# A two-layer streaming step on one core: within-block GLA pairs as 32x32 products in one round, and a new order for the sample tile's turn

## The chip, the cores and the metric

The kernel runs on one core of one Trainium2 chip. The metric is the device time of one execution in microseconds (us), as the median of several runs. TensorE is called PE here, its weight loads PEld, VectorE DVE, ScalarE ACT, GpSimd POOL, and the engine that issues most transfers SP.

## The reference

The model is a step of a hybrid network: 1024 prompt tokens and 8 sampled streams of 16 tokens (1152 tokens, nine tiles of 128) pass through a layer with two recurrences (a gated delta rule and a GLA recurrence), a feed-forward block, a banded attention layer and another feed-forward block. The change touches the two recurrences alone, and of these mostly this part:

```python
def _gla(q, k, v, gk, s0):
    def step(s, inp):
        qc, kc, vc, gc = inp
        b = jnp.cumsum(gc, axis=2)
        o_inter = jnp.einsum('bhcd,bhde->bhce', qc * jnp.exp(b), s)
        diff = b[:, :, :, None, :] - b[:, :, None, :, :]
        decay = jnp.exp(jnp.where(causal[:, :, None], diff, -jnp.inf))
        a = jnp.einsum('bhid,bhjd,bhijd->bhij', qc, kc, decay)
        o = o_inter + jnp.einsum('bhij,bhje->bhie', a, vc)
        blast = b[:, :, -1:, :]
        s = (s * jnp.exp(blast[:, :, 0, :])[..., None]
             + jnp.einsum('bhcd,bhce->bhde', kc * jnp.exp(blast - b), vc))
        return s, o
```

There are 8 heads with 32 key channels and 64 value channels. The decay between two tokens is a product over channels, so `a` isn't one product of two matrices. The kernel splits it into levels.

## The kernel before

**Tiles and turns.** The stage of the recurrences is the function `recurrences`. It works on nine tiles of 128 tokens, the sample tile first (`order`, index 0), then the eight prompt tiles (1 to 8). It is a pipeline in which a turn i does three things at once: it inverts the triangular matrix of tile i and makes its GLA pairs, it prepares tile n = i + 1 (decays, transposes, q-k products), and it finishes tile s = i - 1 (values, outputs, states). The order on each engine is written out by hand in a function `turn`, with a `last_turn` for i = 8, and semaphores (`Tally`) join the engines. Turn 1 is the one in which the sample tile is finished (s = 0). It has eight states, one per stream, and reads them with many small products (`sample_reads`, L3582).

**The inverse.** Per turn there are four levels of blocks of 32: `z_blocks` (L3496) and `du_blocks` (L3503), each 32 products of 32x32, with a copy by ACT between them (`keep_z`) and a merge and a 32x32 transpose by DVE behind them (`put_level`, L4034 and L4036). Then come `z_quarters`, `du_quarters`, `z_half` and `du_half`, with `merge32` (L4046, L4048) and `merge64` (L4052) on DVE. `turn_w` (L3563) uses the finished inverse.

**The GLA pairs.** `exponents(n)` (L3479 to L3485) makes, for each of seven levels (distances 1, 2, 4, 8, 16, 32, 64), the sums of the log decays around a level's middle, and ACT takes their exponentials (`level_exps`). `level_queries` (DVE, L4125) and `level_keys` (POOL, L3395) scale q and k with them. `pairs(k, r)` (L3553) multiplies them in rounds: for each level and for the diagonal (`NL`), eight products of 32 rows, 128 columns of weights and 128 moving columns, one per head, into banks 4 to 7. `place(k, r)` (DVE) puts of each level's 128x128 result only the entries that belong to the level into `gla_pairs`: a masked copy of 128x1024 elements (L4093) for the levels up to 16 and for the diagonal, plain copies (L4090, L4087) for levels 32 and 64. A round holds two levels, as two fit in the banks, so `pairs` of round r + 1 waits for `place` of round r:

```python
rounds_p, rounds_s = [[0, 1], [2, 3], [4, NL], [5, 6]], [[0, 1], [2], [3], [NL]]
```

**The end of a turn** on PE reads: `pairs(i, 0)`, `du_quarters`, `turn_keys`, `turn_qk(n, 2)`, `turn_keys`, `z_half`, `pairs(i, 1)`, `du_half`, `a_pairs(n)`, `pairs(i, 2)`, `p_pairs(n)`, `pairs(i, 3)`, `turn_w`, `exponents(n)`. `turn_keys` (L3702) transposes keys of the attention cache that are on their way through the chip; SP loads and stores them. `smalls(n)` (L3429 to L3434) makes small sums, sixteen of its instructions being the total log decay per head (L3433).

**The stage ahead** is `rest_projection`, whose last group of nine row tiles (L2898) has the first steps of the sample tile between its products (`first_tile`). The first `exponents(0)` and `level_exps(0)` are in turn 0 of the recurrences.

Every fp32 product is two LDWEIGHTS and two MATMUL instructions; the profile counts them singly. An fp32r product is one of each.

Of the kernel before, what the change touches and what calls it, by code (L numbers as in the profile page):

```python
# [21 lines left out]
P = 128  # L22
# [8 lines left out]
GK = 32  # L31
# [20 lines left out]
def shape_constants():  # L52
# [11 lines left out]
    for s in LEVELS:  # L64
# [11 lines left out]
                               for s in LEVELS[:5]], 1)  # L76
# [2505 lines left out]
class FirstTile:  # L2582
# [3 lines left out]
    def __init__(self, load, scale, sums, turn_gla, turn_qk, a_pairs, p_pairs, decays, keep_gla, keep_qk, keep_blocks, factors,  # L2586
                 tiles):
        self.load, self.scale, self.sums, self.turn_gla, self.turn_qk = load, scale, sums, turn_gla, turn_qk
        self.a_pairs, self.p_pairs, self.decays, self.keep_gla, self.keep_qk = a_pairs, p_pairs, decays, keep_gla, keep_qk
        self.keep_blocks, self.factors, self.tiles = keep_blocks, factors, tiles  # L2590


def first_tile(e, ctx, at_):
# [11 lines left out]
    def own(name, shape, spot, dt=F32):  # L2605
# [29 lines left out]
     gla_turned, gla_ready, turned, tready, a_mm, bt_ready, p_mm, pt_ready, btc_ready, zeroed, uc_set, u_put, t_ready) = e.sem(  # L2635
# [3 lines left out]
        "first_p_mm", "first_pt_ready", "first_bt_blocks", "first_zeroed", "first_blocks_set", "first_u_put", "first_t_ready")  # L2639
# [86 lines left out]

    def decays(act):
# [28 lines left out]
    def factors(dve):  # L2756
# [5 lines left out]
        v.tensor_copy(spr[:, 8 * P:9 * P], c("upto_s"))  # L2762
# [19 lines left out]
    return FirstTile(load, scale, sums, turn_gla, turn_qk, a_pairs, p_pairs, decays, keep_gla, keep_qk, keep_blocks, factors,  # L2782
# [3 lines left out]
def rest_projection(e, ctx, hT, raw, out, ws_first, base, done, begin):  # L2786
# [43 lines left out]

    def bank(n):
        return PS[:, 5 + n % 3, :]
# [60 lines left out]
    def tensor(pe):  # L2893
# [22 lines left out]
        def first_step(t):  # L2916
# [9 lines left out]
            if t == 7:  # L2926
                begin.p_pairs(pe)

# [7 lines left out]
        for b in range(4):  # L2936
            for t in range(3 if b == 0 else 0, NT):
                pe.wait_ge(copied, b * NT + t - 2)
# [108 lines left out]
def recurrences(e, ctx, at_, ahead, first):  # L3047
# [11 lines left out]
    rounds_p, rounds_s = [[0, 1], [2, 3], [4, NL], [5, 6]], [[0, 1], [2], [3], [NL]]  # L3059
# [42 lines left out]
    ga = sb("gla_pairs", [P, 2, H, P])  # L3102
    qt = sb("qT", [P, 3, H // 2, P])
# [49 lines left out]
    pairs_mm, ga_put = tally("gla_pairs_mm", 4), tally("gla_pairs_put", 4)  # L3153
# [177 lines left out]
    def gpsimd(pool):  # L3331
# [15 lines left out]
        def scale(k):  # L3347
# [6 lines left out]
            upto = c("upto_s" if sample(k) else "upto_p")  # L3354
# [10 lines left out]
        def decay(k):  # L3365

            if sample(k):
# [5 lines left out]
                go_mm.wait(pool, k)  # L3373
                for m in range(2):
                    x = tt_(GSs[:, m], GSs[:, m], wide(exl[:, k % 3, m], DK), ALU.mult)
                x.then_inc(gsd_ready.sem, 1)
# [12 lines left out]

        def level_keys(k):  # L3390
# [7 lines left out]
        def turn(i, n, s):  # L3398
            if s is not None:
                decay(s)  # L3400
            if n is not None:
                scale(n)
# [9 lines left out]
    def tensor(pe):  # L3412
# [329 lines left out]
        def turn(i, n, s):  # L3742
            if i == NT - 1:
                return last_turn(i, s)
# [1506 lines left out]
```

## Time and profile before

| What | us |
|---|---|
| Median of 3 runs | 3221.96 |
| Lowest and highest run | 3221.78 and 3223.81 |
| The profiled execution | 3232.05 |
| Its span | 3230.4 |

PE is busy 3093.9 us of the span (96%), its weight loads 2905.2 us, DVE 1578.8, POOL 1527.5, ACT 1029.4. The recurrences take from 439.8 us to about 882 us of the span. In the rows of a timeline, the columns are the start, the time from the first start to the last end, the engine, the source line, the operation with its operands and shape, the number of instructions, and in brackets how long the engine stood idle before it and what released it. A row groups instructions of one kind that follow each other.

### The profile page before, as it was taken

How to read it: one execution, taken by the hardware profiler on the slowest of the kernel's cores; microseconds unless marked ns; L12 is line 12 of the kernel's file. 1: busy time of each engine (PE TensorE's matmuls, PEld its weight loads, DVE VectorE, ACT ScalarE, POOL GpSimd, SP SyncE). 2: the span in 40 equal slices, each digit the busy share in tenths (PEclk: the TensorE clock that was granted, in tenths of full speed). 3: DMA queues.
4: the chain of work that ended last, by engine and by line, in shares of the span. 5: the costliest groups of instructions: out<-in, count | busy, mean ns of one | idle time of the engine just before them, and what ended most of it. 6: DMA issues, size and time to landing. Idle time of an engine off the chain costs nothing. (4 is left out here: it accounts for less than half of the span.)

```text
span 3230.4 us, 67257 instructions
## 1 busy us (share of the span) xinstructions
PE 3093.9 (96%) x28484; PEld 2905.2 (90%) x28484; DVE 1578.8 (49%) x2177; ACT 1029.4 (32%) x1834; POOL 1527.5 (47%) x1163
## 2 busy tenths in 40 slices
PE   7999987888898999999999999999999999999999
PEld 6988876777798999999999999877699999999998
DVE  5650034565566545554334433466646445553323
ACT  4222132333434332231212432356624332231112
POOL 4452324344115776674363556311126766764352
PEclk8999988999898999999999999999999999999999
DMA  6222142432651322236423353567521333238342
GB/s 208 83 79 98 59 135 65 146 127 98 212 188 56 97 99 79 94 120 255 146 94 138 93 155 116 171 212 240 155 77 64 103 97 103 78 111 303 98 141 79
DMA packets 371080, 409.45 MB, mean 127 GB/s; under 512 B 29048, under 2 KB 303569, under 8 KB 369768
## 3 DMA queue, kind: packets, MB, share of 16 engines
q1 hardware_dynamic: 363944, 380.24, 35.5%
q0 software_dynamic: 6848, 25.04, 2.5%
q8 instruction: 222, 3.64, 0.5%
q14 instruction: 66, 0.54, 0.1%
HBM read 272.71 MB, written 134.60 MB: 126 GB/s over the span
## 5 line engine op out<-in xcount | busy, mean ns | idle before, releaser
L864 PE MATMUL PS<-token_block,w_block 128*128 128x288 f32 x9408 | 1272.3, 297 | 13.6 <-POOL w_block L778 6.5
L864 PEld LDWEIGHTS PS<-token_block,w_block 128*128 128x128 f32 x9408 | 1264.0, 190 | 16.2 <-POOL w_block L778 6.1
L778 POOL TENSOR_TENSOR w_block<-w_pair_raw,w_block 128x512 fp32r<-128x512 f32 x224 | 303.2, 1360 | 163.2 <-ACT w_block L774 129.2
L1259 PE MATMUL PS<-act_slot,w_down_split 128*128 128x384 f32 x1872 | 330.4, 337 | 6.6 <-DMA act_slot<-act_dram 5.5
L1259 PEld LDWEIGHTS PS<-act_slot,w_down_split 128*128 128x128 f32 x1872 | 328.1, 189 | 8.2 <-DMA act_slot<-act_dram 6.4
L778 POOL TENSOR_TENSOR w_block<-w_sum,w_block 128x512 fp32r<-128x512 f32 x168 | 228.7, 1376 | 96.9 <-ACT w_block L774 96.8
L774 ACT CAST w_block<-w_pair_raw 128x512 fp32r<-128x512 f32 x224 | 137.7, 622 | 306.6 <-PE PS L864 265.2
L774 ACT CAST w_block<-w_sum 128x512 fp32r<-128x512 f32 x168 | 99.5, 621 | 366.2 <-POOL w_sum L767 235.6
L1231 PE MATMUL PS<-token_block,w_block 128*128 128x288 f32 x1344 | 180.4, 296 | 2.1 <-issue 2.1
L1231 PEld LDWEIGHTS PS<-token_block,w_block 128*128 128x128 f32 x1344 | 179.4, 189 | 3.0 <-issue 2.5
L762 POOL TENSOR_TENSOR w_sum<-w_pair_raw 128x512 f32<-128x512 f32 x56 | 87.9, 1570 | 166.4 <-DMA w_pair_raw<-in_ffn_w_gu_dram 112.0
L405 PE MATMUL PS<-hT_high,w_split_tiles 128*128 128x384 f32 x576 | 124.9, 342 | 2.6 <-DVEq L2468 2.6
L1090 POOL CAST w_down_split<-w_down_raw 128x1024 fp32r<-128x1024 f32 (+2 forms) x32 | 28.1, 878 | 207.7 <-PE PS L1259 172.6
L1555 DVE TENSOR_TENSOR xT<-xT,PS 128x1152 f32<-128x1152 f32 x32 | 43.3, 1354 | 155.5 <-PE PS L1259 155.5
L1481 DVE TENSOR_TENSOR u<-p,PS 128x576 f32<-128x576 f32 x44 | 33.1, 752 | 164.9 <-PE PS L864 164.9
L4968 ACT ACTIVATE probs<-minus_scores,minus_max 128x640 f32<-128x640 f32 (+3 forms) x144 | 101.3, 707 | 23.5 <-DVE minus_max L4857 23.2
L1546 DVE TENSOR_TENSOR xT<-xT,PS 128x576 f32<-128x576 f32 x72 | 52.6, 752 | 106.3 <-PE PS L1231 106.3
L3395 POOL TENSOR_TENSOR gla_k_exps<-gla_exps,gla_kT 128x896 f32<-128x896 f32 x18 | 37.1, 2083 | 142.3 <-ACT gla_exps L3820 142.3
L405 PEld LDWEIGHTS PS<-hT_high,w_split_tiles 128*128 128x128 f32 x576 | 101.4, 190 | 2.9 <-POOLq L2338 2.9
L5005 POOL COPY bias_samples<-bias_near 128x384 f32<-128x384 f32 x16 | 8.1, 504 | 195.7 <-DMA bias_near<-near_dram 171.9
L764 POOL TENSOR_TENSOR w_sum<-w_sum,w_pair_raw 128x512 f32<-128x512 f32 x56 | 98.4, 1757 | 4.4
L1497 DVE TENSOR_TENSOR ffn_up<-ffn_up,norm_row 128x1152 f32<-128x1152 f32 x44 | 94.1, 2138 | 4.6
(520 smaller groups left out, 5516.3 us busy)
## 6 DMA issues: line engine op xcount, KB each, us to landing
w_pair_raw<-in_ffn_w_gu_dram SPq DMA_DIRECT2D x88, 512.0 KB, 5.1
act_slot<-act_dram SPq DMA_DIRECT2D x28, 1152.0 KB, 13.0
cache_kT<-kT_dram SPq DMA_DIRECT2D x8, 2048.0 KB, 11.6
cache_v<-in_cache_c_v_dram SPq DMA_DIRECT2D x64, 256.0 KB, 4.8
act_dram<-ffn_act_high SPq DMA_DIRECT2D x28, 576.0 KB, 2.8
act_dram<-ffn_act_low SPq DMA_DIRECT2D x28, 576.0 KB, 3.9
down_source<-down_dram SPq DMA_DIRECT2D x56, 288.0 KB, 5.2
xT<-xT_dram SPq DMA_DIRECT2D x24, 576.0 KB, 12.0
```

The lines of the kernel that those rows point to most:

```text
L405: m = nc.tensor.matmul(PS[:, banks + j, 0:GN], wl if p == 2 else wh, sl if p == 1 else sh, start=(k == first and p == 0), stop=(k == last ...
L762: tt(self.sum_(p, 2), b0, b1, ALU.add).then_inc(self.summed, 1)
L764: tt(self.sum_(p, 1), self.sum_(p, 2), a0, ALU.subtract).then_inc(self.summed, 1)
L774: self.nc.scalar.copy(self.blocks[q][:, 0], self.source(p, q)).then_inc(self.high, 1)
L778: self.nc.gpsimd.tensor_tensor(self.blocks[q][:, 1], self.source(p, q), self.blocks[q][:, 0], ALU.subtract).then_inc(self.low, 1)
L864: m = nc.tensor.matmul(to[:, j], w, x[:, j * HN:(j + 1) * HN], start=(q < 3 and i == 0 and t == 0), stop=(q > 3 and i == 3 and t == 2), sk ...
L1231: m = nc.tensor.matmul(to[:, j], w, x[:, j * HN:(j + 1) * HN], start=(q < 3 and i == 0 and t == 0), stop=(q > 3 and i == 3 and t == 2), sk ...
L1259: m = nc.tensor.matmul(down_banks(u)[:, j], wd[u % 2][:, int(q == 2), k], x[:, int(q == 1), group(j)], start=(k == 0 and q == 0), stop=(k ...
L1497: tt(up[:], up[:], row[:], ALU.mult).then_inc(up_scaled, 1)
L1546: tt(two(x), two(x), down_tile(d, q), ALU.add).then_inc(x_down, 1)
L1555: tt(groups(xT[:, n]), groups(xT[:, n]), down_banks(u), ALU.add).then_inc(x_added, 1)
L4968: nc.scalar.activation(pr[:, g % 2, hp, 0:w], sc[:, hp, 0:w], ACT.Exp, scale=-1.0, bias=mn[:, g % 2, hp, 0:1], accum_out=sm[:, g % 2, hp, ...
```

## The change

Five things change, all in the recurrences and the step before them.

1. **Pairs as blocks.** For the levels 1 to 16 and the diagonal only tokens within the same block of 32 matter. Their products are cut into 32x32 blocks: per level 2 x 4 x 4 = 32 products of 32 rows, 32 weight columns and 32 moving columns instead of 8 products of 32x128x128. Six such levels fit in the banks, so there are two rounds instead of four. DVE merges them by six masked copies of 128x256 into a small tile `gla_pair_blocks` (`gc`), and ACT copies that into the diagonal blocks of `gla_pairs` (`spread_pairs`, four copies of 32x256). The outputs wait for it.
2. **Order of the prompt turns.** `pairs(i, 2)` and `pairs(i, 3)` are gone; `turn_w` stands between `a_pairs` and `p_pairs`.
3. **A turn of its own for the sample tile** (turn 1) on PE, ACT and DVE: the prompt tile's `dec_sums` and `smalls` come between the sample tile's reads of its states; the masked values (`vm`) are made by ACT instead of DVE; the GLA states are multiplied by their decay later in POOL's order.
4. **First exponents.** `exponents(0)` goes to the end of `rest_projection`, behind the last row tile; the last three row tiles use banks 0, 3 and 0.
5. **Small things.** The total log decay per head is one product with ones instead of eight; two of DVE's first fills come later in turn 0.

```diff
-    rounds_p, rounds_s = [[0, 1], [2, 3], [4, NL], [5, 6]], [[0, 1], [2], [3], [NL]]
+    rounds_p, rounds_s = [[0, 1, 2, 3, 4, NL], [5, 6]], [[0, 1, 2, 3], [NL]]
...
         def pairs(k, r):
...
-                    for h in range(4):
-                        rows = slice(GK * h, GK * h + GK)
-                        w, q = (gkt[:, k % 2, m], gqt[:, k % 2, m]) if j == NL else (kl[:, m, j], ql[:, m, j])
-                        y = mm(PS[:, 4 + h, x * 256 + m * P:x * 256 + (m + 1) * P], w[rows], q[rows], start=True, stop=True)
+                    w, q = (gkt[:, k % 2, m], gqt[:, k % 2, m]) if j == NL else (kl[:, m, j], ql[:, m, j])
+                    if j in (NL - 2, NL - 1):
+                        for h in range(4):
+                            rows = slice(GK * h, GK * h + GK)
+                            y = mm(PS[:, 4 + h, x * 256 + m * P:x * 256 + (m + 1) * P], w[rows], q[rows], start=True, stop=True)
+                        continue
+                    for b in range(B):
+                        for h in range(4):
+                            rows = slice(GK * h, GK * h + GK)
+                            y = mm(PS[quad(b), 4 + h, (x * 2 + m) * Q:(x * 2 + m + 1) * Q], w[rows, quad(b)], q[rows, quad(b)],
+                                   start=True, stop=True)
...
         def place(k, r):
...
                 else:
-                    mask = c("up")[:, j * P:(j + 1) * P].rearrange("p (a b t) -> p a b t", a=1, b=1)
-                    y = v.copy_predicated(to, bc(mask, (P, 4, 2, P)), src)
+                    n = min(j, 5)
+                    mask = c("upc")[:, n * Q:(n + 1) * Q].rearrange("p (a b t) -> p a b t", a=1, b=1)
+                    src = PS[:, 4:8, x * 2 * Q:(x + 1) * 2 * Q].rearrange("p h (m t) -> p h m t", m=2)
+                    y = v.copy_predicated(within, bc(mask, (P, 4, 2, Q)), src)
...
+        def spread_pairs(k):
+            ga_put.wait(act, k, 1 if not sample(k) else 2)
+            for b in range(B):
+                x = copy(ga[quad(b), k % 2, :, quad(b)], gc[quad(b)])
+            x.then_inc(ga_spread.sem, 1)
...
         def turn(i, n, s):                      # PE, end of a prompt turn
...
             if n is not None:
                 a_pairs(n)
-            if i is not None:
-                pairs(i, 2)
-            if n is not None:
+            if n is not None and i is not None:
+                turn_w(i)
                 p_pairs(n)
-            if i is not None:
-                pairs(i, 3)
-                turn_w(i)
             if n is not None:
                 exponents(n)
...
+        def sample_turn(i, n, s):               # PE
+            z_blocks(i, 0)
+            sample_values(s)
+            dec_sums(n)
+            du_blocks(i, 0)
+            smalls(n)
+            sample_q_state(s)
+            z_blocks(i, 1)
+            turn_keys(i, 0)
+            du_blocks(i, 1)
+            outputs(s)
+            z_blocks(i, 2)
+            gla_turn(n)
+            du_blocks(i, 2)
+            sample_gla_outputs(s)
+            z_blocks(i, 3)
+            turn_qk(n, 0)
+            sample_dn_states(s)
+            du_blocks(i, 3)
+            turn_keys(i, 1)
+            sample_gla_states(s)
+            z_quarters(i)
+            turn_qk(n, 1)
+            pairs(i, 0)
...
         def smalls(k):
...
-            for h in range(H):
-                r, m = dn_rows(h)
-                mm(PS[r, 3, 16 + m * nb:16 + (m + 1) * nb], gt[:, h:h + 1].broadcast_to((P, DK)), ends, start=True, stop=True)
+            mm(PS[:, 3, 2 * H:3 * H], e.ones, gt, start=True, stop=True)
...
+            if t == 8:                          # PE, rest_projection, behind its last row tile
+                begin.exponents(pe)
...
+            if i == 0:                          # DVE, turn 0, behind put_level(0, 2)
+                v.memset(ga[:], 0.0).then_inc(zeroed, 1)
```

## Rows read from the trace of the kernel before

**Rows 1.** The page: engines' busy time, and the DMA queue of instructions (packets, MB).

```profile
PE 3093.9 (96%) x28484; PEld 2905.2 (90%) x28484; DVE 1578.8 (49%) x2177; ACT 1029.4 (32%) x1834; POOL 1527.5 (47%) x1163
...
q8 instruction: 222, 3.64, 0.5%
```

**Rows 2.** Windows by turn (0, 1, 3, 8): length, busy times (instructions), granted clock, DMA.

```profile
439.79:483.60 43.81, 38.13 (x843) 30.78 (x843) 26.20 (x33) 17.21 (x34) 21.14 (x19) 0.73 0.75 212
483.60:549.64 66.04, 50.04 (x1441) 42.10 (x1439) 31.25 (x47) 17.36 (x36) 23.75 (x19) 0.79 0.25 78
...
594.23:638.66 44.43, 38.73 (x961) 33.16 (x959) 26.75 (x42) 17.28 (x35) 19.55 (x15) 1.00 0.37 122
...
816.43:882.40 65.97, 56.48 (x1021) 51.32 (x1020) 38.13 (x58) 27.96 (x43) 10.59 (x7) 0.79 0.65 216
```

**Rows 3.** Timeline of PE in turn 3.

```profile
594.23 0.75 PE L3496 MATMUL PS<-inverse_blocks,minus_aT_blocks 32*32 32x32 f32 x64
595.61 1.97 PE L3621 MATMUL PS<-v_beta,inverse_T 128*128 128x64 f32 x16 [0.63 <-ACT gla_exps L3820]
...
603.18 0.63 PE L3433 MATMUL PS<-consts_f,dn_log_decay 128*64 128x1 f32 x16
...
619.16 1.17 PE L3553 MATMUL PS<-gla_q_exps,gla_k_exps 32*128 32x128 f32 x32 [0.46 <-DVE gla_state L4162]
...
624.37 1.11 PE L3526 MATMUL PS<-inverse_first_half,minus_aT_odd 64*64 64x64 f32 x16
...
636.42 0.50 PE L3479 MATMUL PS<-spans_r,gla_g_split 128*128 128x512 f32 x1 [0.66 <-DVE gla_pairs L4087]
```

**Rows 4.** Waits of PE in turns 2 to 7: total us, times, longest.

```profile
PE PS L3553 <- DVE gla_pairs L4093: 11.7, 12, 1.4
PE PS L3479 <- DVE gla_pairs L4087: 4.0, 6, 0.7
```

**Rows 5.** Timeline of DVE in turn 3.

```profile
606.45 0.44 DVE L4034 COPY_PREDICATED inverse_T_blocks<-consts_u,PS 128x256 f32<-128x256 uint8 x1
...
622.95 0.83 DVE L4046 COPY inverse_T<-PS 32x256 f32<-32x256 f32 x2
...
629.77 1.20 DVE L4058 SCALAR_TENSOR_TENSOR minus_aT_even<-PS,decay 128x1024 f32<-128x1024 f32 x1
...
635.68 0.68 DVE L4087 COPY gla_pairs<-PS 64x512 f32<-64x512 f32 x1
```

**Rows 6.** Timeline of ACT in turn 3.

```profile
631.00 1.65 ACT L3889 COPY minus_aT_blocks<-minus_aT_even 32x256 f32<-32x256 f32 x4 [4.91 <-DVE minus_aT_even L4058]
```

**Rows 7.** Timeline of PE in turn 1.

```profile
491.38 1.17 PE L3582 MATMUL PS<-dn_states,sample_qT 64*32 64x64 f32 x96 [2.11 <-issue]
492.48 0.58 PE L3496 MATMUL PS<-inverse_blocks,minus_aT_blocks 32*32 32x32 f32 x32
495.39 0.65 PE L3496 MATMUL PS<-inverse_blocks,minus_aT_blocks 32*32 32x32 f32 x32 [2.33 <-issue]
...
527.14 2.09 PE L3553 MATMUL PS<-gla_q_exps,gla_k_exps 32*128 32x128 f32 x32
```

**Rows 8.** DMA of 484 to 500 us: GB/s in 40 slices of 0.4 us; the only queue.

```profile
GB/s 0 0 41 0 0 0 0 0 0 0 0 0 41 0 0 0 0 0 0 0 0 0 41 0 0 0 0 0 0 0 0 41 0 0 0 0 0 0 0 0
...
q8 instruction: 4, 0.07, 1.7%
```

**Rows 9.** A window of 6 us in turn 1, columns as in rows 2.

```profile
493.00:499.00 6.00, 3.67 (x42) 1.99 (x37) 5.70 (x7) 0.37 (x1) 4.76 (x4) 0.50 0.02 5
```

**Rows 10.** Timeline of PE, turn 0.

```profile
439.79 0.74 PE L3496 MATMUL PS<-inverse_blocks,minus_aT_blocks 32*32 32x32 f32 x64 [3.55 <-DVEq L4298]
...
446.85 0.75 PE L3496 MATMUL PS<-inverse_blocks,minus_aT_blocks 32*32 32x32 f32 x64 [1.04 <-DVE inverse_blocks L4036]
```

**Rows 11.** Timeline of PE, turn 8.

```profile
828.54 0.64 PE L3496 MATMUL PS<-inverse_blocks,minus_aT_blocks 32*32 32x32 f32 x50 [0.30 <-issue]
...
833.29 0.31 PE L3503 MATMUL PS<-inverse_T_blocks,z_blocks 32*32 32x32 f32 x11 [0.73 <-issue]
```

More of the change, by code:

```diff
@@ L3353, in scale @@
             tt_(kb[:], kk, wide(col(e.rkb, k), DK), ALU.mult).then_inc(scaled.sem, 1)
-            upto = c("upto_s" if sample(k) else "upto_p")
+            if between:
+                between()
+            upto = c("upto_p")
             dec_exp.wait(pool, k)
@@ L3401, in turn @@
             if n is not None:
-                scale(n)
+                scale(n, (lambda: decay_sample_gla(s)) if s is not None and sample(s) else None)
                 if n + 1 < NT:
@@ L3415, in dec_sums @@
         def dec_sums(k):
-            after = c("after_s" if sample(k) else "after_p")
+            after = c("after_p")
             ug_ready.wait(pe, k)
@@ L3736, in last_turn @@
             ahead.turn(pe, 0)
-            pairs(i, 2)
-            pairs(i, 3)
             turn_w(i)
             ahead.turn(pe, 1)
+        def sample_turn(i, n, s):
[22 more added lines that the diff above has]
+            pairs(i, 0)
+            du_quarters(i)
+            turn_qk(n, 2)
+            turn_keys(i, 2)
+            z_half(i)
+            pairs(i, 1)
+            du_half(i)
+            a_pairs(n)
+            turn_w(i)
+            p_pairs(n)
+            exponents(n)
         def turn(i, n, s):
@@ L3744, in turn @@
                 return last_turn(i, s)
+            if s is not None and sample(s):
+                return sample_turn(i, n, s)
             if i is not None:
                 z_blocks(i, 0)
-            if i == 0:
-                exponents(0)
             if s is not None:
-                (sample_values if sample(s) else values)(s)
+                values(s)
             if i is not None:
@@ L3761, in turn @@
                 du_blocks(i, 1)
-            if s is not None and not sample(s):
+            if s is not None:
                 state(s)
@@ L3970, in turn @@
                 return last_turn(i, s)
+            if s is not None and sample(s):
+                return sample_turn(i, n, s)
             if i is not None:
@@ L4214, in turn @@
                 return last_turn(i, s)
+            if s is not None and sample(s):
+                return sample_turn(i, n, s)
             if i is not None:
@@ L4237, in turn @@
                 factors(n)
-            if s is not None and not sample(s):
+            if s is not None:
                 add_gla_state(s)
```

173 lines of the change are left out of this document (115 added, 58 removed).

## The prediction

> **What bounds the kernel now.** I first read the page: PE is busy 96% of the span [rows 1], so time is won only where PE stands idle or does less. The windows, one per turn of the recurrences, come next [rows 2]. A prompt turn takes 44.43 us, of which PE is busy 38.73, at the full clock (granted 1.00, the level of 2.4 GHz). Turn 0 takes 43.81, turn 1 with the sample tile 66.04 (busy 50.04, clock 0.79), turn 8 65.97. Then the list of PE's waits in the six prompt turns [rows 4]: 11.7 us for `place` behind the rounds of pairs and 4.0 for `place` ahead of `exponents`, 2.6 us a turn. To these comes 0.63 a turn in which the first values wait for the exponentials [rows 3]. Last comes the timeline, to see what each wait hides [rows 3, 5, 6].
>
> One more thing is to be seen in the sample turn. PE stood idle 2.11 and 2.33 us with the releaser "issue", that is, waiting for nothing on another engine [rows 7]. Between the two halts it ran 96 + 32 = 128 matmuls, with as many weight loads: 256 instructions. The page has a DMA queue for instructions with 222 packets and 3.64 MB, 16.4 KB each, and PE ran 2 x 28484 instructions, 257 per packet [rows 1]: one packet is 256 PE instructions. The DMA view of 484 to 500 us shows four such packets and nothing else, in the slices that begin at 484.8, 488.8, 492.8 and 496.4 us [rows 8]. The idle ends at 491.38 and 495.39 [rows 7], about 2.4 us behind the second and third. So PE ran out of instructions. With nothing else on the DMA engines, a new block of 256 came into use after 4.01 us (491.38 to 495.39), though PE had run it in about 1.5.
>
> The Trainium skill (Runtime: NRT & Kernel Launch, Instruction fetch mechanics) also says that instructions come in blocks of 256, but holds that the fetch is hidden because dispatch is slower than the fill, and gives PE room for 2048. The size of the block agrees with the trace; that the fetch is hidden does not agree for dense small matmuls.
>
> **The first round of pairs.** Before, it is 32 matmuls of 32x128, 1.1 us [rows 3]. After, six levels of 32 products, two matmuls each: 384 matmuls and 384 weight loads, 768 instructions, three blocks. The nearest row for their pace is `z_blocks`: 64 matmuls of 32x32 in 0.69 us (0.75 less the tail of the last), 10.8 ns each [rows 3]. At that pace the round takes 4.1 us, and a block 1.37. But a dense run of 256 instructions needs a period T of about 4.0 us [rows 7]. In turn 8, with the DMA engines 65% busy [rows 2], consecutive halts end at 828.54 and 833.29, T = 4.75 [rows 11]. 768 instructions cross three block borders wherever they begin, so they hold two whole periods: P = 4.1 + 2 (T - 1.37). T from 3.7 (a little under the shorter row, as a block may be asked for early) to 4.8 gives P = 8.8 to 11.0. I take T = 4.3, as rows of a tile and of keys travel in this stretch, and P = 10.0.
>
> **Behind it, to `z_half`.** Before, this takes 624.37 - 619.16 = 5.21 us [rows 3]. `z_half` needs `merge32`, which in DVE's order stands behind `place(0)`. After, `place(0)` is six masked copies of 128x256 at 0.48 from start to start, the pace of the row at 606.45 [rows 5]: 2.85 us. `merge32` is 1.25 (two copies 0.83 [rows 5], a third like them 0.42), and 0.1 for signals: P + 4.2 = 14.2, or +9.0 us. `du_quarters`, two `turn_keys` and a `turn_qk` lie on PE beside it and cost nothing more; without that cover they would be about 3.6 us, but DVE's 4.2 would still lead.
>
> **From `z_half` to the next turn.** Before, 638.66 - 624.37 = 14.29 [rows 2, 3]. After, counting from `z_half`: `z_half` 1.04, `pairs(1)` 1.10 (as 619.16's group), `du_half` 1.07, `a_pairs` 1.1 to 4.35. DVE places levels 32 and 64 by 3.75 (two copies of 0.42 and one of 0.68 [rows 5]) and merges until 4.45 (a copy of the same 64x512). `turn_w` runs 4.5 to 5.6. DVE's decayed products (1.20 [rows 5]) end at 5.65, so `p_pairs` runs 5.75 to 6.9, and `exponents` (636.42 to 638.66, 2.24 [rows 2, 3]) to 9.1. DVE's second product (1.2) and the fill, merge and transpose of the next blocks (0.3, 0.45, 0.45, by the 128x256 row) end at 9.35. The next turn starts at 9.45, 4.84 sooner, and its values wait 0.05 instead of 0.63 for the exponentials [rows 3]: together -5.4.
>
> **The clock.** In turn 1 it was at 0.50, the level of 1.2 GHz, from 493 to 499 us [rows 9], right behind the first halt and through the second. In the new round PE is busy 4.1 of 10 us, with two longer halts, so a fall is likely. What it costs can't be read for this place. It isn't under 0, and if all of the 9 us behind the round ran at half clock, work that isn't DVE's or ACT's would cost about 4 more. I take 1.5, as the fall in turn 1 lasted 6 us and part lies in DVE's shadow.
>
> **A prompt turn:** 9.0 - 5.4 + 1.5 = +5.1, six times: +31. Without clock and with T = 3.7 it is +2.4; with T = 4.8 and 4 us of clock +8.6.
>
> **Costs at nothing.** `spread_pairs` adds 1.65 us to ACT, by the four copies of the same size in L3889. ACT is idle 4.91 us before those [rows 6]; without that, up to 1.65 a turn. The shorter `smalls` saves about 0.5 us of PE (0.63 for sixteen matmuls [rows 3]) but the third `z_blocks` waits for DVE's merge at 606.45, which stands right behind the level queries without idle time [rows 5], and these start from the q-state product ahead of `smalls`; 0, at best -0.5 a turn. ACT's added exponential is 0.1 us in an idle stretch; the masks go from DVE to ACT, 2.4 us where both have room. The fills of DVE (2.7 us) move into waits of turn 0.
>
> **Turn 0.** Before, the second `z_blocks` starts 7.06 us after the first [rows 10], as `exponents(0)` and a full set of fills stand between. After, `z_blocks`, copy, `du_blocks`, merge and transpose are 3.6: -3.4. `exponents(0)` now takes about 2.1 us at the end of the stage ahead, where PE is idle 3.55 us anyway [rows 10]; some of the handover stays behind it, +0.6 (0 to 2.1). The sample tile's first round is 512 instructions, two blocks: 6.5 us (4.0 at half clock, one period more) for 2.1, less 0.8 of DVE, +3.6. The shorter end is -3.2, less than in a prompt turn, as the old rounds here hold five levels, not eight. Sum -2.4, from -5 to 0.
>
> **Turn 1.** Up to its first round of pairs it takes 527.14 - 483.60 = 43.5 us [rows 2, 7]. The new order puts slow instructions between the dense reads. PE's own work there is an estimated 25 us (the reads at the 96 in 1.1 us of rows 7, the rest at a prompt turn's durations), and its 2290 instructions are 9 blocks, 9 x 3.8 = 34 if each is bound: I take 34.5, -9. The rest is as in a prompt turn, +3.6 without the clock, which is low here already [rows 2]. Sum -5.4, from -13 to +2.
>
> **Turn 8.** The round adds 8.9, less what DVE saves; the two rounds that go, with their wait, give back about 7: +2, from -3 to +6.
>
> **Sum:** 31 - 2.4 - 5.4 + 2 = +25 on the span of 3230.4. The profiled execution took 3232.05 in all, 10 us over the median of 3221.96; I put the difference on the median: 3247 us. All lower bounds together give 14 - 5 - 13 - 3 = -7, all upper 52 + 0 + 2 + 6 = +60.
>
> **Rivals.** (1) The instructions keep up. Then P = 4.1: a prompt turn is 3.1 - 5.4 = -2.3, six times -14; turn 0 -5, turn 1 -12 as its halts go too, turn 8 -3: 3188 us, faster. For it: before, the prompt turns have the same kind of blocks, and hardly any halt. Against it: their densest run is 128 instructions with slow ones around it, and the halts of rows 7 and 11. It decides for faster once T is under 2.7 us. The rule of the Trainium skill (same page and section) would have this come true; by it there are no halts at all. (2) The sample turn's new order and turn 0 win more than I count (-13 and -5) and T is 3.7 without a clock fall: about 3215 to 3223, no change or slightly faster. For it: 16 us of PE idle in turn 1. (3) The clock stays at 0.50 through the ends of all turns, as turn 0 shows on average (0.73 [rows 2]): +50 and more, 3275 and above.
>
> **Numbers.** Halts as forecast 0.66; rival 1 0.10; rival 2 0.14; rival 3 0.10. Range 3209 to 3278, which leaves out rival 1 and about all of rival 3; the likeliest case's own range is 3230 to 3272. A difference of 0.2%, 6 us, is what can be told from no change. Faster by more: rival 1 and half of rival 2, 0.17. Same: the other half and a bit of the forecast's edge, 0.09. Slower 0.74.
>
> **What would show it.** In a prompt turn after, pairs of 32x32 come as 384 matmuls from start to end in 9 to 11 us, with two idles of 2 to 3 us marked "issue" inside. `z_half` starts some 14 us behind the round's start, the next turn under 10 us later. A prompt turn takes 47 to 50 us, turn 1 about 60. The granted clock of a prompt turn is under 1.00. ACT's copies of pairs end before `bt_blocks` and delay nothing. If the 384 matmuls take 4 to 5 us without idle, the forecast is wrong at its root; if there are halts but a turn is no longer, the end of the turn held more than I read.

## The result, and the profile after

The changed kernel takes 3285.72 us (median of 4 runs, 3281.44 to 3305.81) against 3222.89 us for the kernel before in the same comparison (4 runs, 3221.78 to 3226.67). The ratio is 1.0208, with a 95% interval of 1.0184 to 1.0233: 62.8 us slower, where 25 were forecast and 3278 us was the upper end of the range. The profiled execution took 3288.06 us, its span is 3286.4 us, 56.0 more than the span before. The other 7 us of the 62.8 are there because the profiled execution of before lay 9 us over this median and that of after only 2 us over its own.

The page of the kernel after, the two lines that answer to [rows 1]:

```profile
PE 3108.0 (95%) x30916; PEld 2920.7 (89%) x30916; DVE 1531.2 (47%) x2176; ACT 1046.6 (32%) x1882; POOL 1520.4 (46%) x1163
...
q8 instruction: 241, 3.95, 0.5%
```

DVE does 48 us less than before, and PE's busy time is up by only 14 us, though the span grew by 56. PE executed 2432 matmuls more and fetched 19 blocks of instructions more (2 x 2432 / 256 = 19.0), so the block of 256 instructions named in the prediction is in the numbers. The windows by turn (turns 0, 1, 3 and 4 of after, columns as in [rows 2]; each begins 0.25 us behind the turn's first row, so that turn 3 starts at 607.47 and not at 607.71) show where the 56 us are:

```profile
441.79:487.20 45.41, 36.16 (x1080) 28.98 (x1068) 22.25 (x33) 19.43 (x40) 20.69 (x19) 0.66 0.74 205
487.20:552.75 65.55, 49.03 (x1735) 42.11 (x1724) 21.21 (x45) 22.06 (x45) 21.75 (x19) 0.79 0.25 80
607.71:661.30 53.59, 41.55 (x1257) 35.96 (x1246) 21.99 (x42) 19.25 (x40) 19.52 (x15) 0.84 0.31 96
661.30:710.51 49.21, 40.32 (x1255) 35.02 (x1244) 21.89 (x42) 19.23 (x40) 19.52 (x15) 0.90 0.32 105
```

The six prompt turns 2 to 7 take 49.2 to 55.0 us, 52.2 in the mean, against 44.5. Before, all of them took the same time to 0.2 us; now they differ by 6 us although the work is the same. That points at something that isn't in the kernel's order of work. The timeline of PE in turn 3, the rows that answer to the pairs of [rows 3], shows it:

```profile
632.06 1.54 PE L3578 MATMUL PS<-gla_q_exps,gla_k_exps 32*32 32x32 f32 x161 [0.46 <-DVE gla_state L4273]
635.92 1.53 PE L3578 MATMUL PS<-gla_q_exps,gla_k_exps 32*32 32x32 f32 x128 [2.31 <-issue]
642.39 0.36 PE L3578 MATMUL PS<-gla_q_exps,gla_k_exps 32*32 32x32 f32 x22 [4.94 <-issue]
...
646.12 0.25 PE L3537 MATMUL PS<-inverse_T_blocks,z_blocks 32*32 32x32 f32 x1 [1.97 <-issue]
646.58 1.97 PE L3729 MATMUL PS<-consts_f,sample_wT 128*128 128x128 f32 x8
...
651.61 1.19 PE L3545 MATMUL PS<-inverse_first_half,minus_aT_odd 64*64 64x64 f32 x16
```

PE halts for 2.31 us, runs 128 matmuls with their 128 weight loads, one block, in 1.53 us, and halts again for 4.94 us. Its round of 384 matmuls has borders of blocks at matmul 33, 161 and 289, and halts at the last two. A third halt, 1.97 us, comes at the border behind the round, in `du_quarters`. `z_half` starts at 651.61, 19.55 us behind the first pair. The waits of PE in turns 2 to 7 (releaser, total, times, longest), against [rows 4]:

```profile
PE PS L3578 <- issue: 45.6, 15, 6.0
...
PE PS L3578 <- DVE gla_state L4273: 3.0, 6, 0.7
...
PE PS L3537 <- issue: 2.0, 1, 2.0
PE PS L3538 <- issue: 1.8, 1, 1.8
```

All waits on "issue" in these turns add up to 50.7 us, 8.4 a turn; 49.4 of them are the 17 halts of the three lines shown here. The waits for `place` that the change was to remove (11.7 and 4.0 us) are gone.

One halt in each turn is longer than the others (5.8, 4.9, 3.8, 6.0 and 4.0 us in turns 2 to 6, 2.5 in turn 7). The DMA view of 632 to 652 us, in 40 slices of 0.5 us, says what happened there:

```profile
GB/s 0 0 33 135 172 295 430 397 254 164 131 287 434 422 385 148 49 0 0 0 0 0 0 33 0 0 0 0 0 0 0 0 0 0 0 0 66 401 410 164
...
q8 instruction: 3, 0.05, 1.1%
```

A block of instructions is 33 GB/s in a slice. One stands alone at 633.0. The last one, at 643.5, is alone as well and PE goes on at 646.12, 2.6 us after the slice's start. Between them the engines carry the next tile's rows and the turned keys (qkv 768 KB, two stores of 512 KB, q, k and v) until about 640.5, and the fetch that ends the halt of 4.94 us is in the last slice of that traffic (49 GB/s from 640.0): PE goes on at 642.39, 2.4 us later. Each time PE resumes about 2.5 us after a fetch starts; in the second halt the fetch started late. The row at 642.39 also shows when a fetch can start: the next one is at 643.5, 1.1 us after PE has begun the block before it.

The copies that were costed at nothing are at nothing. ACT in turn 3 copies the pairs to place between 653.44 and 655.09 and is then idle 2.29 us before `bt_blocks`:

```profile
653.44 1.65 ACT L3950 COPY gla_pairs<-gla_pair_blocks 32x256 f32<-32x256 f32 x4
657.37 1.65 ACT L3944 COPY minus_aT_blocks<-minus_aT_even 32x256 f32<-32x256 f32 x4 [2.29 <-DVE minus_aT_even L4164]
```

And DVE's six masked copies take 2.82 us (2.85 forecast), after 11.82 us of waiting for PE:

```profile
643.63 2.82 DVE L4204 COPY_PREDICATED gla_pair_blocks<-consts_u,PS 128x256 f32<-128x256 uint8 x6 [11.82 <-PE PS L3578]
```

### The profile page after: what moved, and what is told of

Its sections match the earlier page's. It is cut to its first block and busy times, and to the rows that moved or that the text cites. A ratio compares the mean times of both kernels' runs of the same rounds, so it can differ in the third digit from the quotient of the medians.

```text
span 3286.4 us, 72152 instructions
## 1 busy us (share of the span) xinstructions
PE 3108.0 (95%) x30916; PEld 2920.7 (89%) x30916; DVE 1531.2 (47%) x2176; ACT 1046.6 (32%) x1882; POOL 1520.4 (46%) x1163
```

## The experiments

The theory (A): small fp32 products issued densely use up a block of 256 instructions in about 1.5 us, while a new block comes every 3.7 us or so and later when data transfers are ahead of it. The halts cost the time, and the rest of the change is a small gain. The rivals: the new orders of turns 0 and 1 (B); something in the array, the banks or the placing (D, E, F); a late fetch for a reason of its own (C1).

**1. `old_rounds`: the change without its pairs.** The pairs, their placing, the four rounds and the end of a prompt turn are as before; the sample tile's turn, the first exponents and the small things are changed.

```diff
-    rounds_p, rounds_s = [[0, 1, 2, 3, 4, NL], [5, 6]], [[0, 1, 2, 3], [NL]]
+    rounds_p, rounds_s = [[0, 1], [2, 3], [4, NL], [5, 6]], [[0, 1], [2], [3], [NL]]
```

> The changed kernel, with the pairs, their placing, their four rounds and the end of a prompt turn as before, so that only the sample tile's turn, the first exponents and the small things are changed. Theory A (the halts for instructions in the dense round cost the time, the rest of the change is a small gain): the prompt turns are back at 44.4 us with a granted clock of 1.00, turn 1 reaches its first round of pairs at about 34 us, and the time is 3211 us (3205 to 3217), that is 12 under the kernel before. Rival B (the new orders of turns 0 and 1 lose time too, through clock or transfers, and carry over into the prompt turns): over 3225 us and prompt turns over 45 us.

Measured: 3209.18 us against 3225.67, ratio 0.995 (0.9935 to 0.9965). Turns 2 to 7 are back at 44.4 to 45.0 us at a clock of 1.00. Turn 1 reaches its first pair after 36.6 us, and after 33.9 in the second profile (34 expected). It was run again in more rounds, for the interval:

> The kernel of old_rounds once more, for a narrower interval: a ratio of 0.995 (0.994 to 0.996) to the kernel before, 3208 us.

Measured: 3210.78 us against 3227.29, ratio 0.9945 (0.9931 to 0.9959). The windows of its turns 0, 1 and 3:

```profile
438.92:478.94 40.02, 32.73 (x824) 25.85 (x827) 26.43 (x34) 17.27 (x35) 20.85 (x19) 0.79 0.83 232
478.94:532.35 53.41, 42.73 (x1433) 36.36 (x1437) 25.94 (x45) 20.37 (x41) 21.77 (x19) 0.94 0.30 97
...
576.77:621.80 45.03, 38.70 (x953) 33.04 (x956) 26.82 (x42) 17.54 (x36) 19.53 (x15) 1.00 0.37 118
```

Turn 0 is 3.8 us shorter than in [rows 2], turn 1 12.6 (9.0 in the first profile, where its clock was 0.82 instead of 0.94). Rival B falls: those parts gain about 0.5%, and this kernel beats both.

**2. `blocks_in_before`: the pairs alone,** with their placing and the new end of a prompt turn, in the kernel before.

```diff
-    rounds_p, rounds_s = [[0, 1], [2, 3], [4, NL], [5, 6]], [[0, 1], [2], [3], [NL]]
+    rounds_p, rounds_s = [[0, 1, 2, 3, 4, NL], [5, 6]], [[0, 1, 2, 3], [NL]]
```

> The kernel before, with only the 32x32 pairs in one round, their placing through the small tile, and the new end of a prompt turn. Theory A: prompt turns of about 52 us, first rounds of 10 to 15 us with three halts a turn, and since the gain of turns 0 and 1 (about 12 us) is missing, 3297 us (3288 to 3306). Rival B: as the sample turn's order is the old one, the time is under that of the changed kernel, 3286.

Measured: 3302.18 us, ratio 1.0234 (1.0217 to 1.0251), prompt turns of 48.0 to 58.8 us, 53.1 in the mean. As expected. The two halves of the change, +2.34% and -0.5%, add up to 1.8%, nearly its 2.08%.

**3. `late_loads`: another order of SP's transfers.**

```diff
-            if n is not None and n + 1 < NT:
-                load_qk(n + 1)
-                load_v(n + 1)
             c_ = i if i is not None else -1
             for x in units(c_):
                 store_keys(x)
+            if n is not None and n + 1 < NT:
+                load_qk(n + 1)
+                load_v(n + 1)
```

> The changed kernel, with SP's loads of the next tile (qkv, q and k, v; 1.28 MB) issued behind the stores of the turned keys instead of ahead of them. Theory A1 (the second fetch of instructions in the round comes late because it stands behind these transfers): the second halt of the first round falls from about 5 to about 2.4 us, a prompt turn loses 2 to 3 us, and the time is 3268 us (3262 to 3277). Rival C1 (the fetch is late for a reason of its own, not for the transfers): halts as they were, 3286 within 5. A second rival, C2: the loads come too late for the next tile's scaling and a new wait eats the gain.

Measured: 3272.16 us, ratio 1.0145 (1.0118 to 1.0172), where the changed kernel has 1.0208 (1.0184 to 1.0233). In turns 2 to 7 the round's halts fell from 45.6 to 33.3 us, and the longest from 6.0 to 3.6. The timeline of PE in turn 3, all rows with a halt, and under it the DMA view of 621 to 641 us in slices of 0.5:

```profile
624.78 1.53 PE L3578 MATMUL PS<-gla_q_exps,gla_k_exps 32*32 32x32 f32 x128 [2.18 <-issue]
628.23 0.36 PE L3578 MATMUL PS<-gla_q_exps,gla_k_exps 32*32 32x32 f32 x22 [1.92 <-issue]
631.96 0.26 PE L3537 MATMUL PS<-inverse_T_blocks,z_blocks 32*32 32x32 f32 x1 [1.98 <-issue]
```

```profile
GB/s 25 0 33 0 0 0 0 0 0 33 0 0 0 0 0 0 33 0 0 0 0 0 0 0 0 0 0 0 0 0 188 410 410 66 0 8 139 410 369 217
```

With the data out of the way, the fetches stand 3.5 us apart and the halt of 4.94 us is one of 1.92. C1 falls. C2 falls too: the list of PE's waits in turns 2 to 7 has none for a transfer. A prompt turn takes 50.9 us in the mean, 1.4 less and not the 2 to 3 expected; turns 0 and 1 give another 5.2. The halts themselves stay: the transfers only made them longer.

**4. `diagonal_order`: another order of the products.**

```diff
-                    for b in range(B):
-                        for h in range(4):
-                            rows = slice(GK * h, GK * h + GK)
+                    for z in range(4 * B):
+                            h, b = z % 4, (z + z // 4) % B
+                            rows = slice(GK * h, GK * h + GK)
```

> The changed kernel, with the 16 products of 32x32 of each half level in another order: each next product takes another row group, column group and bank, where before four products in a row share the output columns. Theory A (the fetch sets the length of the round): 384 matmuls still take 10 to 15 us with halts at the same borders, 3286 us within 6. Rival D (the array or the banks hold up the small products): the round gets shorter by 2 us or more a turn, under 3274 us, or longer by as much.

Measured: 3294.06 us (3283.24 to 3301.91), ratio 1.0218 (1.0192 to 1.0245), not to be told from the changed kernel by the ratio, though 8 us over its median and not within the 6 expected. The rounds of turns 1 to 8 took 9.4 to 14.2 us (9.8 to 15.9 in the changed kernel). D falls as far as this order can show it.

**5. `twice_the_products`: the first round twice.**

```diff
-            for x, j in enumerate(jobs):
+            for x, j in [*enumerate(jobs)] * (2 if r == 0 else 1):
```

> The changed kernel with every product of the first round of pairs issued twice, one whole set after the other: 768 matmuls or 1536 instructions, three blocks of 256 more in turns 1 to 8 and two more in turn 0. Theory A (a block costs the period of its fetch, 4.0 to 5.0 us): each first round gets 12 to 15 us longer, turn 0 by 8 to 10, the time is 3403 us (3380 to 3430). Rival G (the halts are a fixed cost of the round and further products run at 10.8 ns each): 4.1 us a round more, 3323 us.

Measured: 3379.41 us (one run), 91.3 more than the changed kernel's profiled execution for 26 blocks more (267 packets of instructions for 241): 3.5 us a block. Rival G, 1.37 us a block, falls; the forecast of 12 to 15 us a round was high (9.3 to 12.1 in turns 1 to 7), and the time lies 0.6 us under the expected range. The timeline of PE in turn 3, all halts of its round:

```profile
665.44 1.27 PE L3578 MATMUL PS<-gla_q_exps,gla_k_exps 32*32 32x32 f32 x128 [2.08 <-issue]
672.47 0.37 PE L3578 MATMUL PS<-gla_q_exps,gla_k_exps 32*32 32x32 f32 x22 [5.75 <-issue]
676.20 1.53 PE L3578 MATMUL PS<-gla_q_exps,gla_k_exps 32*32 32x32 f32 x128 [2.20 <-issue]
679.93 1.53 PE L3578 MATMUL PS<-gla_q_exps,gla_k_exps 32*32 32x32 f32 x128 [2.20 <-issue]
683.67 0.37 PE L3578 MATMUL PS<-gla_q_exps,gla_k_exps 32*32 32x32 f32 x22 [2.20 <-issue]
```

This is the cleanest reading of the period: 672.47, 676.20, 679.93, 683.67. Behind the one fetch that stood behind data (5.75 us of halt), with the DMA engines otherwise empty, blocks follow each other every 3.73 us: 1.53 of work and 2.20 of halt. It isn't one fixed number, though: the next block is in use 3.45 us later (687.12, in `du_quarters`), and in the other turns of this run and of experiment 3 the blocks behind each other on empty engines come after 3.46, 3.74 or 4.02 us.

**6. `four_rounds_of_blocks`: the same products in four rounds.** The rounds and the order on PE and DVE are as before, the form of the products is the new one; ACT's copies of the pairs come behind `keep_w`.

```diff
-    rounds_p, rounds_s = [[0, 1, 2, 3, 4, NL], [5, 6]], [[0, 1, 2, 3], [NL]]
+    rounds_p, rounds_s = [[0, 1], [2, 3], [4, NL], [5, 6]], [[0, 1], [2], [3], [NL]]
```

> The changed kernel with as many products of 32x32 (levels 1 to 16 and the diagonal), but in four rounds of two levels at the places that the rounds had before, with slow work between them. The longest dense stretch of small products is then 128 matmuls, not 384. Theory A (a dense stretch outruns the instructions; the number of instructions in a whole turn, about 2500 or 9.8 blocks at 4.0 us, still fits in 44): the halts shrink to under 3 us a turn, prompt turns of 44.5 to 47 us, 3220 us (3208 to 3235). Rival E (each small product costs wherever it stands, or the placing through the small tile does): prompt turns stay at 50 us and more, over 3260 us.

Measured: 3289.0 us (3274.56 to 3298.2), ratio 1.0185 (1.0159 to 1.0211). I was wrong by 69 us, and Rival E's number came true. The halts did fall, as theory A has it, from 8.4 to 4.6 us a turn, but the turns stayed long. The windows of its turns 2 and 4:

```profile
548.10:609.93 61.83, 50.34 (x1234) 43.56 (x1232) 23.02 (x42) 19.27 (x40) 18.74 (x15) 0.78 0.36 109
...
666.32:716.30 49.98, 42.44 (x1234) 36.73 (x1232) 22.00 (x42) 19.05 (x40) 19.53 (x15) 0.90 0.31 103
```

The same 1234 matmuls take 50.34 us of busy time in one turn and 42.44 in another, by the clock (0.78 and 0.90). In the mean PE is busy 47.0 us a turn, 8.7 more than the 38.3 of experiment 1; the 288 more matmuls make some 3 of that at 10.8 ns each, and an estimated 6 are left for the clock. That was the gap in theory A: it counted the halts and not what follows them. The products cost that much here wherever they stood, so this run alone does not refute E; experiments 7, 8 and 9 were for that.

**7. `two_levels`: few products.** PE leaves out the products of levels 4, 8, 16 and of the diagonal (the placing stays).

```diff
             for x, j in enumerate(jobs):
+                if r == 0 and j not in (0, 1):
+                    continue
```

> The changed kernel in which PE multiplies only the two lowest levels in the first round: the products of levels 4, 8, 16 and of the diagonal are left out (their placing by VectorE and the copies by ScalarE stay, and work on what stood there). Theory A: without the dense stretch there is at most half a halt a turn, the time from the first pair to z_half is 5.6 to 6.5 us (DVE's six masked copies and merge32), a prompt turn 39.5 to 41.5 us, the granted clock 1.00, the time about 3180 us. Rival F (the placing, the copies by ACT or the new end of the turn cost the time, not the products): prompt turns over 44 us, over 3205 us.

Measured: 3224.36 us (one run). That is 44 us more than theory A's number and inside F's, and the turns take 44.4 us in the mean where 39.5 to 41.5 were expected. The single turns tell why. Turn 4, the only one without a halt, takes 39.65 us at a clock of 1.00, just as theory A has it, and 5.69 us from first pair to `z_half`. So placing, copies and the new end are innocent, against F. The other five have 2.1 to 3.2 us of halts each and take 42.5 to 48.1. What failed is "at most half a halt a turn": 128 matmuls of pairs and the 48 of `du_quarters` are still enough for one. Turn 5 shows most of what can follow, with a single halt. Its PE timeline, and under it windows from 694.7 to 707 us:

```profile
694.57 1.09 PE L3580 MATMUL PS<-gla_q_exps,gla_k_exps 32*32 32x32 f32 x107 [0.47 <-DVE gla_state L4275]
698.17 0.33 PE L3580 MATMUL PS<-gla_q_exps,gla_k_exps 32*32 32x32 f32 x12 [2.52 <-issue]
699.32 1.97 PE L3731 MATMUL PS<-consts_f,sample_wT 128*128 128x128 f32 x8
...
704.35 1.97 PE L3545 MATMUL PS<-inverse_first_half,minus_aT_odd 64*64 64x64 f32 x16
```

```profile
694.70:698.00 3.30, 0.96 (x107) 0.85 (x101) 0.00 (x0) 2.62 (x7) 3.22 (x5) 0.98 0.50 159
698.00:701.00 3.00, 2.83 (x77) 2.76 (x78) 2.19 (x5) 0.00 (x0) 0.27 (x1) 0.50 0.74 203
701.00:704.00 3.00, 2.66 (x14) 2.29 (x12) 1.62 (x5) 1.50 (x2) 0.00 (x0) 0.50 0.87 342
704.00:707.00 3.00, 3.00 (x30) 2.55 (x33) 0.00 (x0) 1.64 (x3) 0.00 (x0) 0.50 0.44 169
```

The clock is at its full level up to the halt of 2.52 us and at 0.50, the level of 1.2 GHz, right behind it; the transposes take 1.97 us instead of the 1.09 of turn 4, `z_half` 1.97 instead of 1.11 [rows 3]. It stays there until about 715. The turn takes 48.14 us, 8.5 more than turn 4: 2.5 are the halt, 6.0 the clock. Turns 5 and 7 (47.87 us) are the dear ones; turns 2, 3 and 6 cost 2.8 to 4.8 us over turn 4. The clock fell behind the halts of turns 3 and 6 too (2.12 us until 616.33, 2.54 us until 746.69), but for less long:

```profile
616.00:619.00 3.00, 2.67 (x26) 2.61 (x27) 1.96 (x5) 0.21 (x1) 0.19 (x1) 0.50 0.91 268
620.00:624.00 4.00, 4.00 (x71) 3.65 (x72) 0.73 (x2) 3.12 (x7) 0.00 (x0) 1.00 0.67 259
...
746.00:752.00 6.00, 4.97 (x51) 4.54 (x52) 2.07 (x5) 1.50 (x2) 0.41 (x1) 0.50 0.79 279
753.00:757.00 4.00, 3.90 (x75) 3.45 (x73) 2.15 (x5) 2.80 (x6) 0.00 (x0) 1.00 0.66 200
```

Turn 3 takes 2.8 us more than turn 4, turn 6 takes 4.1 more. So a halt of 2.5 us cost 4.1 in one turn and 8.5 in another; why the clock came back so much later in turn 5 stays open.

**8. `idle_before_pairs`: an idle stretch without small products.** The kernel of experiment 1, with idle time of PE that has nothing to do with instructions.

```diff
+            if i is not None and i > 1 and s is not None:
+                for m, l in ((0, NL), (1, 3)):
+                    tt_(ql[:, m, 0:l], ex[:, m, 0:l], over_heads(gqt[:, i % 2, m], l), ALU.mult)
             if s is not None:
                 add_gla_state(s)
```

> The kernel of old_rounds (no 32x32 pairs, no halts for instructions in prompt turns), in which VectorE repeats part of its level queries (1.47 + 0.63 us, the same values again) ahead of the GLA state's update in the turns 2 to 7. PE then stands idle about 2.6 us ahead of its first round of pairs instead of 0.5, in a stretch of slow instructions. Theory K (a stretch of idle PE of this length brings the granted clock to the 1.2 GHz level by itself, and the slow end of the turn then costs more than the idle): turns 2 to 7 last 44.4 + 2.1 + 3 to 8 us, with a granted clock under 0.95, in all 3245 us (3235 to 3265). Rival L (the clock falls only where small products run dense, or the fetch itself is what lowers it): 46.5 us a turn at a clock of 1.00, 3222 us.

Measured: 3243.07 us (2 runs), ratio 1.0044 (1.0027 to 1.0061). PE's idle time ahead of the pairs is 3.63 us instead of 0.46. The first row of the round in turn 3, and three windows from there on:

```profile
610.22 2.05 PE L3572 MATMUL PS<-gla_q_exps,gla_k_exps 32*128 32x128 f32 x32 [3.63 <-DVE gla_state L4269]
```

```profile
606.50:610.20 3.70, 0.08 (x1) 0.02 (x1) 3.42 (x6) 3.28 (x8) 3.70 (x4) 1.00 0.18 42
610.20:612.00 1.80, 1.78 (x32) 1.77 (x32) 0.00 (x0) 0.00 (x0) 1.64 (x3) 0.53 0.98 349
612.00:614.00 2.00, 2.00 (x59) 1.74 (x53) 1.66 (x2) 0.00 (x0) 0.00 (x0) 0.50 0.75 191
```

The clock falls behind this idle stretch too, and is back at 1.00 by 618. Turns 2 to 7 take 49.94 us in the mean against 44.52 in the second profile of experiment 1, +5.4, of which 3.2 are the added idle time; the other 2.3, 1.9 of it between first pair and `z_half`, are put down to the clock (3 to 8 were expected). Rival L falls: an idle PE in front of slow products is enough, without small ones and without a halt for instructions. (32.3 us between the two medians, 6 x 5.4 = 32.5.)

**9. `half_the_instructions`: bfloat16.** The levels' scaled q and k are in bfloat16, with less exact values; the diagonal stays in fp32.

```diff
-    ql = sb("gla_q_exps", [P, 2, NL, P])
-    kl = sb("gla_k_exps", [P, 2, NL, P])
+    ql = sb("gla_q_exps", [P, 2, NL, P], mybir.dt.bfloat16)
+    kl = sb("gla_k_exps", [P, 2, NL, P], mybir.dt.bfloat16)
```

> The changed kernel with the scaled q and k of the levels held in bfloat16, so that a product of two levels is one LDWEIGHTS and one MATMUL instead of two of each; the diagonal stays in fp32, and the values are less exact. Same number of products, same round, same places, same order. A prompt turn's first round falls from 768 to 448 instructions (1.75 blocks). Theory A (instructions, not products, set the round): one or two halts a turn instead of three, first pair to z_half 7 to 10 us instead of 18.2, a prompt turn 41 to 46 us, in all 3218 us (3200 to 3235). Rival E (the number of small products, the placing or the copies by ACT set it): prompt turns over 49 us, over 3260 us.

Measured: 3241.59 us (3226.5 to 3244.32), ratio 1.0038 (1.0022 to 1.0055). Halts fell to 4.9 us a turn, first pair to `z_half` from 18.2 to 12.5, a prompt turn to 47.1. It missed the expected time by 24 us and lies between A's numbers and E's: the halts are as few as expected, one or two long ones a turn, but up to 4.7 us long, and the clock is low again (0.80 to 0.93). Turn 5 has one halt:

```profile
709.06 1.45 PE L3578 MATMUL PS<-gla_q_exps,gla_k_exps 32*32 32x32 bf16 x160 [0.46 <-DVE gla_state L4273]
...
713.07 0.74 PE L3578 MATMUL PS<-gla_qT,gla_kT 32*32 32x32 f32 x49 [2.42 <-issue]
```

With 448 instructions instead of 768 for the same 192 products, most of the loss is gone (+0.4% for +2.1%). Of the 5.7 us between first pair and `z_half`, 3.5 are halts; that speaks for the instructions and against E. The rest isn't separated: 160 matmuls less are also up to 1.7 us less of PE's own work (at 10.8 ns each), and bfloat16 products of 128 columns are shorter as well: `z_half` to the next turn is 9.03 us in four of the six turns, not 9.39. The values of `pairs` are less exact, so this is no version to keep.

**10. `three_rounds`: a version meant to win.** Levels 1, 2 and 4 as blocks, and three rounds.

```diff
-    rounds_p, rounds_s = [[0, 1, 2, 3, 4, NL], [5, 6]], [[0, 1, 2, 3], [NL]]
+    rounds_p, rounds_s, BLOCKED = [[0, 1, 2, 5], [6, 3], [4, NL]], [[0, 1, 2], [3], [NL]], (0, 1, 2)
```

> A mixed form: levels 1, 2 and 4 as 32x32 blocks with level 32 in one round, then levels 64 and 8, then level 16 and the diagonal, the last three of these as 128x128 products; ScalarE copies the small tile's blocks to place before the other levels are placed. A prompt turn has 144 more matmuls than before, not 288, and its longest dense stretch is 208 + 48. Theory A: one halt of 1 to 2.5 us a turn; the first pair to z_half 6.4 us and the halt, z_half to the next turn 10.5 instead of 14.3: prompt turns of 42 to 44 us, 3201 us (3190 to 3215). Rival H: two halts a turn and a lower clock take all of it back, 45 us and more a turn, over 3215 us.

Measured: 3246.83 us (3240.72 to 3257.36), ratio 1.0063 (1.0046 to 1.0079). H is right. Turns 2 to 7 take 45.6 to 57.8 us; the halts are 4.1 us a turn, and four of the six turns have a clock of 0.96 or 0.93, two 0.79 and 0.81. A round of 208 matmuls of which 192 are small still crosses a border of a block at full pace, and that is enough.

## Why the prediction was wrong, point by point

The direction and the mechanism hold; the size doesn't, and the time lies 8 us above the range. Half of the miss is in the prompt turns, the other half in turns 0, 1 and 8, where the forecast was too low as well. By the profiles, starts of turns 0, 1, 2 and 8 (their first `z_blocks` row) at 441.54, 486.95, 552.51 and 865.99 us against 439.79, 483.60, 549.64 and 816.43:

| Term of the sum | Forecast | Measured |
|---|---|---|
| Turn 0 with the handover | -2.4 | +3.4 (start +1.8, turn +1.6) |
| Turn 1 | -5.4 | -0.5 |
| Six prompt turns | +31 | +46.7 |
| Turn 8 and behind it | +2 | +6.4 |
| Sum | +25 | +56.0 |

**The prompt turns: the number of halts, and the second one's length.** "768 instructions cross three block borders wherever they begin, so they hold two whole periods" is the step that failed. Two whole periods do lie between three borders, but a halt can stand at the first border as well (3.27 us in turn 2), and at a fourth behind the round, as `du_quarters` is 48 more small matmuls (1.97 and 1.81 us in turns 3 and 6). In the six turns there are 17 halts, 2.8 a turn, not 2. That alone makes the 2.5 us a turn: the 17 halts last 2.90 us in the mean, and the forecast gave each 2.93 (4.3 - 1.37). But this mean is luck, as it mixes halts of 0.6 and 6.0 us. T isn't one number: 3.45 to 4.02 us on empty DMA engines (the 3.7 to 4.0 of the forecast was good), but 6.5 from 635.92 to 642.39 (and up to 7.3 in other turns), when the fetch stood behind a tile's rows and the keys. The bound of 4.8 was taken from turn 8, and was too low for transfers issued together. In numbers: halts 8.4 us a turn for the forecast's 2 x (4.3 - 1.37) = 5.9, all but 0.1 of them between first pair and `z_half`. The round itself took 10.1 to 15.9 us, 11.9 in the mean, where P = 10.0 stood. First pair to `z_half` took 18.2 us, not 14.2 and a part of the 1.5 for the clock.

**Behind the round and the end of the turn: right.** 18.2 less 8.35 of halts is 9.8, of which the forecast's pace and DVE's work make 4.1 + 4.2; 1.5 are left for the clock and for what it stretches behind the third halt, and 1.5 stood in the forecast. From `z_half` to the next turn it takes 9.39 to 9.44 us in all six turns (9.45 forecast, 14.29 before). ACT's copies, the masks and the fills cost nothing, as said.

**The clock of a prompt turn: right, for a reason that was not seen.** It was below 1.00 in each (0.84 to 0.90), but it cost only about 1.5 us, since in the changed kernel it falls in the middle of halts, and in turn 3 is back at 1.00 from 652 us on. This is an argument from the rows and what is left of a sum, not a measurement: of 6 us from 640 to 646 PE was busy for 1.76 at 0.50. Once the products are spread over four rounds (experiment 6), the halts are shorter and the low clock meets work at full price: what the halts give back, the clock takes. Why it fell again in some stretches of experiment 6 without any halt there stays open.

**Turn 1: the new order is as forecast, its round isn't.** It reaches its first pair after 33.99 us (34.5 forecast, 43.54 before). Then first pair to `z_half` takes 17.79 (before 7.30) and the end 13.77 (before 15.20), in sum +9.1 where +3.6 stood. The end ran at the low clock; in experiment 3 it took 9.37. The round has halts of 9.2 us where 5.9 stood, one of them of 6.30 us behind the next tile's rows and the keys. "Without the clock, which is low here already" was wrong: the new order without the new round had raised it (0.82 and 0.94 in the two profiles of experiment 1, 0.79 before), and the round brought it down again to 0.79.

**Turn 0.** The head gave 4.0 us (3.4 forecast), the round cost 7.9 from first pair to `z_half` (3.6 forecast), the end gave 2.3 (3.2 forecast). The round itself took 6.2 us (6.5 forecast); what was missing in the sum is a second halt of 2.00 us behind it, inside `turn_keys`, and a clock of 0.50 until about 478 us. The start 1.8 us later is no property of the change: kernels with the same step ahead started this turn anywhere from 438.5 to 443.0 us.

**Turn 8.** +6.4, just over the upper end of its range, with halts of 7.1 us for 5.0 before.

**The rivals.** Rival 1, that the instructions keep up, would have given 3188 us; experiments 5 and 9 exclude it. The rule of the Trainium skill that stood behind it (Runtime: NRT & Kernel Launch, Instruction fetch mechanics), that crossing a block's boundary is mostly hidden, does not agree with the 2.20 us of halt at three borders in a row in experiment 5. Rival 2 had the size of the sample turn's gain about right (-9.0 to -12.6 in experiment 1, where the new round is absent), but with the round that gain is eaten up. Rival 3, the low clock through the ends of all turns, wasn't it either: in this run only turns 1 and 8 ran most of their ends at the low clock, turn 8 before the change as well, and the ends of the prompt turns went as forecast.

The best version found is that of experiment 1, 0.5% faster than before: the sample turn's order, the first exponents and the small things, with the pairs as they were. That leaves 44.4 us a prompt turn. The 39.65 us of experiment 7's turn 4 show what the new placing and the new end could be worth with few enough instructions.

## What to carry to other kernels

Count instructions as a resource of its own. Before cutting a product into smaller ones, divide the instructions of the new stretch by 256 and set the result against its time: here a block took 3.45 to 4.02 us to come on empty DMA engines, so by estimate a stretch of several blocks with more than some 64 to 74 PE instructions per us (256 / 4.02, 256 / 3.45) ends in halts, whatever PE could do, and whatever the average over the turn says. Then look at what transfers are issued just ahead of the dense stretch, and at what work stands behind it, for part of it runs at the low clock: in experiment 7 a halt of 2.5 us cost 4.1 us in one turn and 8.5 in another.

## What the runs showed of the hardware that was not expected

- The fetch of a block starts 1.0 to 1.1 us after PE has begun the block before it, and PE goes on 2.3 to 2.7 us after that start. In a dense stretch on empty DMA engines the blocks come every 3.45 to 4.02 us (experiments 3 and 5). The fetch waits behind data transfers that were issued before it (halts up to 6.8 us, in turn 1 of experiment 9), and moving these transfers shortens it (experiment 3).
- 160 bfloat16 matmuls of 32x32, with as many weight loads beside them, ran in 1.45 us, about 9 ns each (experiment 9), less than half of the 3.45 us in which a block can come: the products themselves are not what holds the dense round up.
- One idle stretch brought the granted clock from 1.00 to 0.50, behind halts for instructions of 2.1 to 2.5 us (experiment 7) and behind a wait of 3.6 us for VectorE (experiment 8). How long it stayed at 0.50 differed much: about 3.5, 6.5 and 16 us in turns 3, 6 and 5 of experiment 7, behind halts of 2.12, 2.54 and 2.52 us. The same kernel's turns differ by up to 8 us for that.
